# The last down projection with tokens on the partitions, the keys' logarithms on another engine, and an earlier first transpose

## The chip, the cores and the metric

The kernel runs on one core of one Trainium2 chip. The metric is the device time of one execution in microseconds (us); less is better. The core's engines run side by side and meet at semaphores only: TensorE (PE in the profile, its weight loads PEld), VectorE (DVE), ScalarE (ACT), GpSimd (POOL), and SyncE (SP), which issues all DMAs here. TensorE writes to PSUM (eight banks of 512 float32 columns on 128 partitions); VectorE and ScalarE read it.

## The reference, cut to what matters

Two layers of a streaming encoder, over 1024 prompt tokens and 8 x 16 sample tokens (1152 in all, `TOK`), width 1024. What the change touches is the end, and one step of the first mixer:

```python
# ab_mixer (layer 0)
log_f = jnp.logaddexp(jnp.log(lb), jnp.log1p(-lb) + jax.nn.log_sigmoid(fz))
k = (1.0 - lb) * jax.nn.sigmoid(-fz)
...
# conv_ffn, the last part of each layer; D_FF = 2816
y = jnp.einsum('btf,fd->btd', jax.nn.gelu(conv, approximate=False) * gate, w_out)
...
x = x + f.astype(x.dtype)            # residual
...
y = rms_norm(x, norm_final)          # x * rsqrt(mean(x*x) + EPS) * gain, float32
```

With one even layer the lower bound is zero, so the kernel computes log f = min(z,0) - ln(1+exp(-|z|)) and k = exp(log f - z).

## The kernel before, in words

**Layout.** Activations stand transposed: features on the partitions, tokens along them, in three blocks (`NTB`) of 384 tokens (`TB`). The residual is `xs` (eight feature slices of 128). All large products are made of three matmuls of split operands: a rounded high part and a low part (the rest), high x high, high x low, low x high. Activations have `xh`/`xl` or `yh`/`yl`, weights `wh`/`wl`.

**A weight piece** is 128 x 512 values. It goes through a ring of four `raw` buffers: SP loads it (line 422) once the low part of the piece four before is made; POOL multiplies a norm's gain into it (line 2537), or only counts it where there is no gain; ScalarE makes the high part (`high`, line 1974) when TensorE has passed a given tick; VectorE makes the low part (`low`, line 1232). `wh` and `wl` have two places each. TensorE waits for both. A piece of a unit feeds 36 matmuls of 384 columns.

**Order.** Each engine has one program written out by hand; `PLAN` only counts pieces, PSUM groups and ticks so that the semaphore numbers agree. Six banks take the groups in turn; banks 6 and 7 serve norms and small transposes.

**The start.** SP issues three token tiles (`xtok`, tokens on the partitions), then seven small DMAs with the gains as rows (`vrow`), the first pieces, then more tiles. TensorE waits for all seven, turns the tiles with transposes (line 715), and after the fourth group turns the rows into `vec`, which POOL needs for scaling weights.

**The keys.** In the first projection (`ab`) a loop over units j evicts the products on VectorE. At j = 5 VectorE forms `logf` for two halves (line 1314, 128 x 2304 each). POOL subtracts z from it (`log_keys`, line 2581), queued behind its scalings for j = 7. At j = 6 and 7 VectorE scans them (`decay`).

**The end.** The conv-FFN of layer 1 loops over steps of 256 features: four units up (two convolved and gated), one down into `xs`. The last two steps are left to `last_down` (line 683), whose contraction has two halves: `yh`/`yl` and `yh2`/`yl2`. For each quarter of the output features it makes two slices of 128 features by 384 tokens in three groups each. VectorE adds each group to `xs` (line 1245), ScalarE squares it (line 1988), POOL adds the squares into `ssq_b` (line 2543). Then comes the final norm: TensorE sums over the partitions with a matrix of ones (line 697), ScalarE takes the root (line 1993), VectorE the reciprocal (line 1960) and multiplies `xs` by it and by the gain (line 1963). TensorE turns the result (line 1223), ScalarE copies it to `otok` (line 2512), which has two places, and SP stores 128 tokens at a time (line 595). Between them the tails of the convolution are turned (line 1110), copied (`tail_rows`) and stored.

Of the kernel before, what the change touches and what calls it, by code (L numbers as in the profile page):

```python
# [23 lines left out]
P = 128  # L24
# [22 lines left out]
V_MIX, V_FFN, V_FIN, V_OUTG, V_PSC, V_LNG, V_LNB, NVEC = 0, 16, 32, 40, 41, 45, 61, 77  # L47
# [18 lines left out]
for _l in range(2):  # L66
# [10 lines left out]
    PLAN.add(f"f{_l}9", 8, 24, 28)  # L77
PLAN.add("out", 0, 18, 18)
# [3 lines left out]
def build(nc, A, O):  # L82
    ctx = ExitStack()
    with ctx:  # L84
# [38 lines left out]
        y_normed = sem("y_normed")  # L123
# [225 lines left out]
        otok = at("otok", [P, 2, D], F32, slot(8))  # L349

# [4 lines left out]
        def tbs(tb):  # L355
            return slice(tb * TB, (tb + 1) * TB)

# [59 lines left out]
        def _(sp):  # L417
# [17 lines left out]
            def x_tiles(tb):  # L435
                for t in range(3 * tb, 3 * tb + 3):
# [4 lines left out]
                    (V_FIN, A["norm_final"].rearrange("(k p) -> k p", p=P)),  # L441
# [56 lines left out]
            def ffn(l):  # L498
# [27 lines left out]
                n0, _, _ = PLAN.at[f"f{l}9"]  # L526
                last_down(wfo[l], n0, FJ - 4)
# [83 lines left out]
        def _(pe):  # L611
# [94 lines left out]
            pe.wait_ge(rows_loaded, 16 * 7)  # L706
# [371 lines left out]
            def ffn(l):  # L1078
# [22 lines left out]
                n2, g2, _ = PLAN.at[f"f{l}9"]  # L1101
                last_down(n2, g2, done0 + 2 * STEPS, yh2, yl2)

            def turn_tails(l):

                pe.wait_ge(conv_step[l], 9 * FJ)
                pe.wait_ge(rms_ready, NTB * (3 + 2 * l))
# [101 lines left out]
            norm(4, ssq_b)  # L1209
            turn_tails(1)  # L1210

            _, g0, _ = PLAN.at["out"]
            for t in range(NT):
                pe.wait_ge(y_normed, KD * (t // NTB + 1))
                for b in range(2):
                    m = 2 * t + b
                    if m < BANKS:
                        bank = acc_bank(g0 + m, g0 + m)
                    else:
                        pe.wait_ge(y_out, m - (BANKS - 1))  # L1220
                        bank = ps[(g0 + m) % BANKS]
                    for k in range(4):
                        mm = pe.transpose(bank[:, k * P:(k + 1) * P], xs[:, 4 * b + k, t * P:(t + 1) * P], ident[:, :])  # L1223
                    mm.then_inc(pe_tick, 1)
# [3 lines left out]
        def _(dve):  # L1228
            def low(n, s):

                dve.wait_ge(w_high_ready, n + 1)
                dve.tensor_tensor(wl[:, s % 2, :], raw[:, s % RAWS, :], wh[:, s % 2, :].bitcast(F32), ALU.subtract)\  # L1232
                    .then_inc(w_low_ready, 1)
# [81 lines left out]

            def decay(c):
# [1483 lines left out]
```

## Time and profile before

| | |
|---|---|
| median of 3 runs | 3001.09 us (2999.42 to 3002.92) |
| the profiled execution | 3001.59 us, its span 2999.9 us |
| mean granted TensorE clock | 0.985 of full speed |
| TensorE busy | 2876.5 us (96%) |
| VectorE, GpSimd, ScalarE busy | 1558.8, 797.1, 719.0 us |
| DMA | 130.19 MB, 43 GB/s on average |

The span is the time from the first to the last instruction; the execution takes 1.7 us more. Busy time is a sum over the whole kernel and says nothing on where an engine is waited for; for that there are the chain of waits, followed back from the last instruction, and the order of time with the idle time ahead of an instruction in square brackets. Recorded matmul durations overlap, since matmuls are pipelined: 0.69 us are recorded for three of 384 columns, but the next three start 0.52 us later.

### The profile page before, as it was taken

To read this page: it belongs to the slowest core of one execution; us is meant where nothing else is said; L and a number is where in the kernel's file an instruction comes from. 1 tells how busy PE (TensorE), PEld (TensorE's weight loads), DVE (VectorE), ACT (ScalarE), POOL (GpSimd) and SP (SyncE) were. 2 spreads that over 40 slices of the span, in tenths; PEclk is the share of its full clock that TensorE was granted. 3 is DMA by queue.
4 is the path that set the end of the run, shared out by engine and by line. 5 is a ranking of instruction groups with operands and counts; after the bars stand their busy time and mean duration, and the time that the engine had idled before them with its cause. 6 is when DMAs were issued, how large, how long until landed. Compare 5 with 4: busy or idle time off the path is not lost. (4 is left out here: it accounts for less than half of the span.)

```text
span 2999.9 us, 45868 instructions
## 1 busy us (share of the span) xinstructions
PE 2876.5 (96%) x16647; PEld 2823.8 (94%) x16647; DVE 1558.8 (52%) x2787; ACT 719.0 (24%) x1143; POOL 797.1 (27%) x603
## 2 busy tenths in 40 slices
PE   8998987999999999999999999999999999999997
PEld 8898887999999999999999889999999999999996
DVE  4557875454444444446544875555544444444454
ACT  4424453321111111113211211213311111111123
POOL 3233324322222222223211230002422222222223
PEclk9998999999999999999999999999999999999998
DMA  4111001111111111111221101111111111111111
GB/s 138 35 33 45 22 15 32 45 39 43 42 42 38 38 42 42 42 42 39 55 66 42 36 30 42 42 42 39 46 41 40 42 42 39 42 42 42 39 43 70
DMA packets 208066, 130.19 MB, mean 43 GB/s; under 512 B 8851, under 2 KB 205156, under 8 KB 207716
## 3 DMA queue, kind: packets, MB, share of 16 engines
q1 hardware_dynamic: 207972, 128.92, 14.3%
q8 instruction: 61, 1.00, 0.1%
q14 instruction: 33, 0.27, 0.0%
HBM read 120.08 MB, written 8.81 MB: 43 GB/s over the span
## 5 line engine op out<-in xcount | busy, mean ns | idle before, releaser
L634 PE MATMUL bank<-xh,wh 128*128 128x384 f32 x3048 | 701.1, 337 | 27.5 <-DVE wl L1232 26.0
L634 PE MATMUL bank<-xl,wh 128*128 128x384 f32 x3048 | 692.5, 334 | 0.0
L634 PE MATMUL bank<-xh,wl 128*128 128x384 f32 x3048 | 692.4, 334 | 0.0
L2537 POOL TENSOR_TENSOR raw<-raw,vec 128x512 f32<-128x512 f32 x280 | 299.1, 1079 | 1389.2 <-DMA raw<-in_w_in_ffn 897.1
L1974 ACT ACTIVATE wh<-raw 128x512 fp32r<-128x512 f32 x414 | 260.4, 629 | 1654.5 <-PE bank L634 1005.7
L634 PEld LDWEIGHTS bank<-xh,wh 128*128 128x128 f32 x3048 | 539.2, 188 | 43.9 <-issue 40.4
L1232 DVE TENSOR_TENSOR wl<-raw,wh 128x512 fp32r<-128x512 f32 x414 | 322.5, 779 | 474.9 <-ACT wh L1974 474.8
L634 PEld LDWEIGHTS bank<-xl,wh 128*128 128x128 f32 x3048 | 543.6, 188 | 0.0
L634 PEld LDWEIGHTS bank<-xh,wl 128*128 128x128 f32 x3048 | 543.6, 188 | 0.0
L1245 DVE TENSOR_TENSOR xs<-bank,xs 128x384 f32<-128x384 f32 (+1 forms) x672 | 332.8, 550 | 309.4 <-PE bank L659 256.1
L659 PE MATMUL bank<-yh,wh 128*128 128x384 f32 x1152 | 267.6, 340 | 5.5 <-DVE xs L1245 2.8
L659 PE MATMUL bank<-yl,wh 128*128 128x384 f32 x1152 | 266.3, 339 | 0.0
L659 PE MATMUL bank<-yh,wl 128*128 128x384 f32 x1152 | 266.2, 339 | 0.0
L659 PEld LDWEIGHTS bank<-yh,wh 128*128 128x128 f32 x1152 | 208.9, 189 | 6.8 <-issue 6.0
L659 PEld LDWEIGHTS bank<-yh,wl 128*128 128x128 f32 x1152 | 208.7, 189 | 0.0
L659 PEld LDWEIGHTS bank<-yl,wh 128*128 128x128 f32 x1152 | 208.6, 189 | 0.0
L2677 POOL TENSOR_TENSOR gate<-gate,cv 128x1152 f32<-128x1152 f32 x40 | 115.5, 2889 | 234.9 <-DVE xs L1245 212.0
L1238 DVE TENSOR_TENSOR gate<-bank,rstd 128x384 f32<-128x384 f32 x132 | 65.4, 551 | 194.0 <-PE bank L634 194.0
L1238 DVE TENSOR_TENSOR apad<-bank,rstd 128x384 f32<-128x384 f32 x88 | 45.0, 553 | 177.6 <-PE bank L634 177.6
L2543 POOL TENSOR_TENSOR ssq_b<-ssq_b,sq_b 128x384 f32<-128x384 f32 x72 | 82.0, 1139 | 132.5 <-ACT sq_b L1988 124.1
L2683 POOL TENSOR_TENSOR yl<-gate,yh 128x1152 fp32r<-128x1152 f32 x40 | 114.8, 2892 | 0.0
L1700 DVE SCALAR_TENSOR_TENSOR cv<-apad,convc,cv 128x1024 f32<-128x1024 f32 x88 | 112.5, 1278 | 0.0
(263 smaller groups left out, 2972.3 us busy)
## 6 DMA issues: line engine op xcount, KB each, us to landing
raw<-in_w_in_ffn SPq DMA_DIRECT2D x176, 256.0 KB, 2.9
raw<-in_w_out_ffn SPq DMA_DIRECT2D x88, 256.0 KB, 2.6
raw<-in_w_uv_c SPq DMA_DIRECT2D x64, 256.0 KB, 2.8
raw<-in_w_in_ab SPq DMA_DIRECT2D x40, 256.0 KB, 2.9
raw<-in_w_out_c SPq DMA_DIRECT2D x32, 256.0 KB, 2.6
xtok<-in_x_prompt SPq DMA_DIRECT2D x8, 512.0 KB, 6.1
raw<-in_w_out_ab SPq DMA_DIRECT2D x16, 256.0 KB, 2.7
out_y_prompt<-otok SPq DMA_DIRECT2D x8, 512.0 KB, 2.8
```

The costliest lines, as they stand in the source:

```text
L634: mm = pe.matmul(ps[(sg + tb) % BANKS][:, 0:TB], w[:, place, k * P:(k + 1) * P], r[:, kk, tbs(tb)], start=kk == 0 and c == 0, stop=kk == K ...
L659: mm = pe.matmul(ps[(sg + g0 + tb) % BANKS][:, 0:TB], w[:, place, k * 256 + dd * P:k * 256 + (dd + 1) * P], r[:, k, tbs(tb)], start=k == 0 ...
L1232: dve.tensor_tensor(wl[:, s % 2, :], raw[:, s % RAWS, :], wh[:, s % 2, :].bitcast(F32), ALU.subtract)\
L1238: dve.tensor_tensor(dst, ps[bank % BANKS][:, 0:TB], rstd[:, tbs(tb)], ALU.mult)\
L1245: dve.tensor_tensor(xs[:, d, tbs(tb)], ps[sg % BANKS][:, 0:TB], xs[:, d, tbs(tb)], ALU.add)\
L1700: dve.scalar_tensor_tensor(outp, padp[:, j:j + SEQ], col(16 + j), outp, ALU.mult, ALU.add)\
L1974: act.activation(wh[:, s % 2, :], raw[:, s % RAWS, :], ACT.Copy).then_inc(w_high_ready, 1)
L2537: pool.tensor_tensor(r, r, g, ALU.mult).then_inc(w_scaled, 1)
L2543: pool.tensor_tensor(ssq[:, tbs(tb)], ssq[:, tbs(tb)], sq[:, par, :], ALU.add)\
L2677: pool.tensor_tensor(gate[:, c, :], gate[:, c, :], cv[:, c, :], ALU.mult)\
L2683: pool.tensor_tensor(yl[:, c, :], gate[:, c, :], yh[:, c, :].bitcast(F32), ALU.subtract)\
```

## The change

1. The last down projection (layer 1) swaps its operands: a slice of 128 tokens of `yh`/`yl` is the stationary operand, a weight piece of 128 x 512 the moving one, and the product has tokens on the partitions. There are nine token tiles with two column halves each, 18 groups of 12 matmuls. All eight weight pieces are kept (`fin_h`, `fin_l`, `wh`, `wl`, `fin_h2`, `fin_l2`). The first eight groups go over eight banks with their first contraction half, then with their second; the other ten go one after the other.
2. The residual is added in PSUM: four float32 matmuls with a slice of `xs` as the stationary operand and the identity as the moving one, into the same group.
3. The final norm goes by token: ScalarE squares each group with an accumulated sum, two tiny steps make the root, VectorE takes the reciprocal of 128 x 1 and multiplies the PSUM group by it and by the gain along the columns (`fin_gain`, one DMA to all partitions) into `otok`. The additions to `xs`, the squares on `ssq_b`, the norm's matmuls, the scaling of `xs`, the transposes and the copies of before are gone.
4. The tails of layer 1 are turned ahead of the projection instead of behind the norm.
5. `log_keys` is on VectorE at j = 6, between two low parts, instead of on POOL at j = 7.
6. TensorE no longer waits for the rows before the first transpose, only before it turns them; the row of the final gains is not loaded there.

```diff
@@ PLAN @@
-    PLAN.add(f"f{_l}9", 8, 24, 28)
-PLAN.add("out", 0, 18, 18)
+    if _l == 0:
+        PLAN.add("f09", 8, 24, 28)
+PLAN.add("fin", 8, 18, 18)
...
+        FIN_BANKS = tuple((FIN_G + e) % BANKS for e in range(3)) + (6,) + \
+            tuple((FIN_G + e) % BANKS for e in range(3, 6)) + (7,)
@@ sync @@
+                for p in range(8):
+                    a, b, k = p // 4, p // 2 % 2, p % 2
+                    load_piece(FIN_N + p, wfo[1][:, FJ - 4 + 2 * a + k:FJ - 3 + 2 * a + k, b * 512:(b + 1) * 512],
+                               FIN_N + p)
+                sp.wait_ge(pe_tick, FIN_T)
+                sp.dma_start(fin_gain[:, :], A["norm_final"].rearrange("(o d) -> o d", o=1).to_broadcast([P, D]))\
+                    .then_inc(fin_gain_loaded, 16)
@@ tensor, start @@
             pe.wait_ge(ident_ready, 1)
-            pe.wait_ge(rows_loaded, 16 * 7)
...
                 if g == 3:
-                    pe.wait_ge(rows_loaded, 16 * 7)
+                    pe.wait_ge(rows_loaded, 16 * 6)
@@ tensor, end @@
             ffn(1)
-            norm(4, ssq_b)
             turn_tails(1)
...
+            def fin_part(m, a):
+
+                t, b = divmod(m, 2)
+                bank = ps[FIN_BANKS[m % 8]]
...
+                sh, sl = ((yh, yl), (yh2, yl2))[a]
+                for k in range(2):
+                    p = 4 * a + 2 * b + k
...
+                    for c, (w, r) in enumerate(((hi, sh), (hi, sl), (lo, sh))):
...
+                        mm = pe.matmul(bank[:, :], r[:, k, t * P:(t + 1) * P], w,
+                                       start=a == k == c == 0, stop=a == k == 1 and c == 2)
+                return mm
...
+            def fin_residual(m):
...
+                for k in range(4):
+                    pe.matmul(bank[:, k * P:(k + 1) * P], xs[:, 4 * b + k, t * P:(t + 1) * P], ident[:, :],
+                              start=False, stop=False)
+
+            for m in range(8):
+                fin_part(m, 0)
+                fin_residual(m)
+            for m in range(8):
+                fin_part(m, 1).then_inc(pe_tick, 1)
+            for m in range(8, 2 * NT):
+                fin_part(m, 0)
+                fin_residual(m)
+                fin_part(m, 1).then_inc(pe_tick, 1)
@@ vector @@
+                if j == 6:
+                    log_keys(0)
+                    log_keys(1)
                 low(2 * j + 2, 2 * j + 2)
...
-                        low(n + 2 * u + 2, sn + 2 * u + 2)
+                        if l and u == 3 and isinstance(s, int) and s:
+                            for p in range(4):
+                                fin_low(p)
...
+            dve.wait_ge(fin_gain_loaded, 16)
+            for t in range(NT):
+                dve.wait_ge(fin_rms, t + 1)
+                inv = fin_sums[:, t, 2:3]
+                dve.reciprocal(inv, inv).then_inc(fin_inv, 1)
+                if t >= 2:
+                    dve.wait_ge(y_stored[t % 2], 16 * (t // 2))
+                dve.wait_ge(fin_inv, t + 1)
+                for b in range(2):
+                    c = slice(b * 512, (b + 1) * 512)
+                    dve.scalar_tensor_tensor(otok[:, t % 2, c], ps[FIN_BANKS[(2 * t + b) % 8]][:, :], inv,
+                                             fin_gain[:, c], ALU.mult, ALU.mult).then_inc(y_out, 1)
@@ scalar @@
+                        for p in range(4):
+                            fin_high(p, 0)
+                        fin_high(4, tick + 13)
+                        y_high(s, yh2, (0,))
+                        fin_high(5, tick + 16)
+                        tail_rows(1)
+                        y_high(s, yh2, (1,))
+                        fin_high(6, tick + 16)
+                        fin_high(7, tick + 16)
...
                 for b in range(2):
                     m = 2 * t + b
+                    act.wait_ge(pe_tick, FIN_T + m + 1)
+                    if m:
+                        act.wait_ge(fin_squared, m)
+                    act.activation(fin_sq[:, :], ps[FIN_BANKS[m % 8]][:, :], ACT.Square,
+                                   accum_out=fin_sums[:, t, b:b + 1]).then_inc(fin_squared, 1)
+                act.wait_ge(fin_squared, 2 * t + 2)
+                act.activation(fin_sums[:, t, 3:4], fin_sums[:, t, 1:2], ACT.Identity, bias=eps_c, scale=1.0 / D)\
+                    .then_inc(fin_bias, 1)
+                act.wait_ge(fin_bias, t + 1)
+                act.activation(fin_sums[:, t, 2:3], fin_sums[:, t, 0:1], ACT.Sqrt, bias=fin_sums[:, t, 3:4],
+                               scale=1.0 / D).then_inc(fin_rms, 1)
@@ gpsimd @@
-                if j == 7:
-                    log_keys(0)
-                    log_keys(1)
```

## Rows read from the trace of the kernel before

**Rows 1.** The page: head, and busy us, share and instructions of TensorE.
```profile
span 2999.9 us, 45868 instructions
...
PE 2876.5 (96%) x16647; PEld 2823.8 (94%) x16647; DVE 1558.8 (52%) x2787; ACT 719.0 (24%) x1143; POOL 797.1 (27%) x603
```

**Rows 2.** The chain that ended last, from 2900 us: start, us, what.
```profile
2910.68 46.87 PE bank L683 x268
...
2971.48 4.32 DVE xs L1963 x8
```

**Rows 3.** TensorE in order of time, the last projection: start, us, instructions.
```profile
2910.52 0.69 PE L683 MATMUL bank<-yh,wh 128*128 128x384 f32 x3
...
2960.32 0.69 PE L683 MATMUL bank<-yh,wl 128*128 128x384 f32 x3
```

**Rows 4.** All engines in order of time, the keys in the first projection.
```profile
101.11 5.02 DVE L1314 SCALAR_TENSOR_TENSOR work<-work 128x2304 f32<-128x2304 f32 x2
...
103.73 12.80 POOL L2581 TENSOR_TENSOR work<-work 128x2304 f32<-128x2304 f32 x2 [10.47 <-DVE work L1314]
...
106.04 11.04 DVE L1232 TENSOR_TENSOR wl<-raw,wh 128x512 fp32r<-128x512 f32 x2
...
111.71 1.30 PE L634 MATMUL bank<-xh,wh 128*128 128x384 f32 x3 [5.46 <-DVE wl L1232]
...
119.65 0.68 PE L634 MATMUL bank<-xh,wh 128*128 128x384 f32 x3
```

**Rows 5.** All engines in order of time, the start.
```profile
8.44 2.79 PE L715 MATMUL bank<-ident,xtok 128*128 128x128 f32 x12 [8.44 <-DMA vrow<-in_c_ln_bias]
...
16.00 0.61 PE L715 MATMUL bank<-ident,xtok 128*128 128x128 f32 x3
```

**Rows 6.** TensorE in order of time, four plain float32 products inside a unit.
```profile
247.42 1.11 PE L876 MATMUL bank<-work,ones 128*128 128x128 f32 x8
248.28 0.77 PE L788 MATMUL bank<-xh,wh 128*128 128x384 f32 x3
248.89 0.34 PE L788 MATMUL bank<-xl,wh 128*128 128x384 f32 x1
```

**Rows 7.** ScalarE's groups by line and shape: busy us, mean ns | idle before.
```profile
L1988 ACT ACTIVATE sq_b<-xs 128x384 f32<-128x384 f32 x72 | 35.9, 519 | 41.9 <-POOL ssq_b L2543 22.0 <-DVE xs L1245 19.9
...
L2512 ACT ACTIVATE otok<-bank 128x512 f32<-128x512 f32 x18 | 10.3, 596 | 13.1 <-PE bank L1223 7.9 <-DMA out_y_prompt<-otok 5.0
...
L1993 ACT ACT_TABLE_LOAD x5 | 6.4, 1283 | 0.1
...
L2007 ACT ACTIVATION_READ_ACCUMULATOR xsq<-xtok 128x1 f32 x9 | 1.8, 202 | 0.0
L2140 ACT ACTIVATE ebp<-work 128x4 f32<-128x4 f32 x8 | 1.6, 196 | 0.0
```

**Rows 8.** Line 1483 alone: duration ns min/median/max, first and last start.
```profile
L1483 DVE SCALAR_TENSOR_TENSOR work<-work,vec x9: 743/751/1214, 252.5 to 470.7; 128x512 f32<-128x512 f32 x9
```

**Rows 9.** All engines in order of time, ScalarE's last copies.
```profile
2995.68 1.09 ACT L2512 ACTIVATE otok<-bank 128x512 f32<-128x512 f32 x2
```

**Rows 10.** VectorE in order of time, in the last gated unit.
```profile
2905.21 0.69 DVE L1232 TENSOR_TENSOR wl<-raw,wh 128x512 fp32r<-128x512 f32 x1 [5.16 <-ACT wh L1974]
```

**Rows 11.** Token tiles' DMAs, issued before 3 us and from 6 to 9 us.
```profile
L437 SPq DMA_DIRECT2D xtok<-in_x_prompt x3: 397/421/432, 0.8 to 1.7; - x3
...
DMA to landing us min/median/max: 3.7/4.5/5.5
...
L437 SPq DMA_DIRECT2D xtok<-in_x_prompt x3: 432/433/758, 6.1 to 7.4; - x3
...
DMA to landing us min/median/max: 5.7/6.5/7.8
```

**Rows 12.** The recurrence's stretch: length, busy us (count), granted clock, DMA share, GB/s.
```profile
200.00:500.00 300.00, 256.27 (x1643) 242.54 (x1642) 220.77 (x352) 139.09 (x274) 107.22 (x89) 0.93 0.10 29
```

**Rows 13.** TensorE's weight loads by line and shape: those of the last transposes.
```profile
L1223 PEld LDWEIGHTS bank<-ident,xs 128*128 128x128 f32 x72 | 12.4, 197 | 9.1 <-DVE xs L1963 9.1
```

More of the change, by code:

```diff
@@ L1638, in _, with finish_down @@
                 abo(i)
-            def finish_down(n0, g0, t0, k, last):
+            def finish_down(n0, g0, t0, k):
                 def lows(d):
-                    if not last:
-                        for tb in range(NTB):
-                            x_low(24 * k + NTB * d + tb, d, tb)
+                    for tb in range(NTB):
+                        x_low(24 * k + NTB * d + tb, d, tb)
                 def adds(d):
@@ L1759, in ffn @@
                 y_last(1)
-                n2, g2, t2 = PLAN.at[f"f{l}9"]
-                finish_down(n2, g2, t2, 2 + 2 * l, l == 1)
+                if l == 0:
+                    n2, g2, t2 = PLAN.at["f09"]
+                    finish_down(n2, g2, t2, 2)
+                else:
+                    for p in range(5, 8):
+                        fin_low(p)
             ffn(0)
@@ L2318, in _, with finish_down @@
                 abo(i)
[L2320 removed]
+            def finish_down(n0, g0, t0, k):
                 for q in range(4):
@@ L2323, in finish_down @@
                         p = n0 + 2 * q + dd + 2
-                        if p < PIECES:
-                            high(p, p, t0 + 7 * q + (7 if dd else 1))
+                        high(p, p, t0 + 7 * q + (7 if dd else 1))
                         for tb in range(NTB):
                             m = 6 * q + NTB * dd + tb
-                            finished(24 * k + m, 2 * q + dd, tb, g0 + m, sq_b, not last)
+                            finished(24 * k + m, 2 * q + dd, tb, g0 + m, sq_b)
                         for tb in range(NTB):
@@ L2357, in ups @@
                             gelu(1, 2 * s + 1)
-                        if p >= 8 and isinstance(s, int) and s:
-                            y_high(s, yh2, (p - 8,))
+                    if not isinstance(s, int) or s == 0:
+                        high(n + 8, sn + 8, tick + 13)
+                        high(n + 9, sn + 9, tick + 16)
+                    elif l == 0:
+                        for c in range(2):
+                            high(n + 8 + c, sn + 8 + c, tick + 13 + 3 * c)
+                            y_high(s, yh2, (c,))
+                    else:
+                        for p in range(4):
[7 more added lines that the diff above has]
+                        fin_high(7, tick + 16)
                 n0, g0, t0 = PLAN.at[f"f{l}0"]
@@ L2707, in ffn @@
                         y_low(STEPS - 2)
-                n2, _, _ = PLAN.at[f"f{l}9"]
-                linked(pool.memset(ssq_b[:, :], 0.0))
-                scale_weights(n2, 0, 4, None)
-                scale_weights(n2 + 1, 0, 4, None)
-                finish_down(n2, 2 + 2 * l, V_MIX + KD if l == 0 else None)
+                if l == 0:
+                    n2, _, _ = PLAN.at["f09"]
+                    linked(pool.memset(ssq_b[:, :], 0.0))
+                    scale_weights(n2, 0, 4, None)
+                    scale_weights(n2 + 1, 0, 4, None)
+                    finish_down(n2, 2, V_MIX + KD)
+                else:
+                    for p in range(8):
+                        scale_weights(FIN_N + p, 0, 4, None)
             ffn(0)
```

143 lines of the change are left out of this document (83 added, 60 removed).

## The prediction

> **What bounds the kernel now.** I read the page's busy times first: TensorE is busy for 2876.5 us of a span of 2999.9 us [rows 1]. So only two kinds of place can give much: where TensorE idles, and what comes after its last real product. Second, the chain of waits over the last 100 us: the last down projection (the matmuls of line 683) is one unbroken TensorE piece up to 2957.6 us, and behind it comes a chain through every engine in turn: squares, POOL's sums, one reciprocal and eight scalings (4.3 us together) for each of three token blocks, transposes, copies, stores [rows 2]. Third, I read the order of time around the projection: it starts at 2910.52 us, its last three matmuls start at 2960.32 us [rows 3]. With 0.52 us for those three it is over at 2960.84 us, so 39.1 us of the span are the tail. Last, the waits of TensorE before 510 us, which led to the two other places of the diff: 5.46 us at 111.7 us, ended by VectorE's low part of a weight piece [rows 4], and 8.44 us at the very start, ended by the DMA of the last small row of gains [rows 5].
>
> **The last projection, part by part.** Before, it is 288 matmuls of 384 columns in 50.32 us [rows 3], 174.7 ns each. 384 columns at the granted full clock of 2.4 GHz are 160.0 ns, so 14.7 ns come on top. After, 18 groups (9 token tiles, 2 column halves) have 12 matmuls of 512 columns each: 216, with the same 110592 columns. No row shows this kind of operand 512 wide. From below the columns alone give 213.3 ns, 46.1 us in all; from above, an excess in proportion gives 232.9 ns, 50.3 us. I take the excess as fixed for each matmul, since each has its own weight load in both: 213.3 + 14.7 = 228.0 ns, 49.3 us.
>
> The residual comes back as TensorE work: 18 x 4 products of 128 columns in plain float32. The nearest row is a group of four plain float32 products of 128 columns (eight records, since each takes two passes): from 247.42 to 248.28 us, 0.86 us for four [rows 6]. 18 x 0.86 = 15.5 us. Behind those four the next three wide matmuls took 0.61 us (248.28 to 248.89) rather than 0.52: a switch costs 0 to 0.09 us. I take half, 18 x 0.045 = 0.8 us. The four turned tails of the convolution move ahead of the projection: about four times 0.11 us from the same row, 0.45 us. The norm's three products and the 72 output transposes go; they lay wholly in the tail.
>
> Sum on TensorE: 0.45 + 49.3 + 15.5 + 0.8 = 66.05 us, so its stream ends at 2910.52 + 66.05 = 2976.6 us. Its drain shows as the difference between 0.69 us recorded for three and 0.52 us of pace [rows 3]: 0.17 us.
>
> Behind the last group stands this chain, for one token tile of 128 only. ScalarE squares 512 columns of PSUM (a copy of that form 0.60 us) and reads its accumulator (0.20 us); two tiny ScalarE steps, each as the 128 x 4 form at 0.20 us [rows 7], each with some 0.05 us to the next by the gaps in the chain; a tiny reciprocal, which I price the same, 0.2; two VectorE steps of 512 columns, for which the row of that form gives a median of 0.75 us [rows 8], with 0.05 for what a read of PSUM may add; then the store. The last of ScalarE's copies of before ends at 2996.77 us and the span at 2999.9 us [rows 1, 9]: 3.1 us. Together 0.17 + 0.85 + 0.50 + 0.2 + 1.55 + 3.1 = 6.4 us. New end 2983.0 us, 16.9 us earlier.
>
> What hides the rest: the eight weight pieces now need eight highs and lows that mostly sit earlier, four of them within the last gated unit. There VectorE's next low comes only at 2905.2 us, after 5.16 us of idleness [rows 10]; four lows are 4 x 0.69 = 2.8 us. On ScalarE the four highs need no tick; the fourth also needs its transfer, which can leave only when the low ahead of that idleness is done, at 2900.0 us, so even with the 5.5 us that a far larger transfer took to land at the start [rows 11] it ends before 2907 us, and TensorE wants that piece at about 2913 us: 6 us of cover. Behind the waiting fourth low are queued the product for the last gate, and behind ScalarE's fourth high its rounding; they need to be ready only when the second half of the contraction starts, eight groups (8 x 2.27 = 18 us) after 2910.5. The broadcast of the final gains on SP stands behind all weight loads and is 20 us early. The tail copies of ScalarE (0.76 us for four) delay the last highs by that much, inside the same 18 us. For each token tile ScalarE needs about 2.3 us and VectorE 1.8 us, beside 2.7 us of TensorE for two groups in the opening eight and 7.2 us later, so neither becomes the bound; the store of tile t-2 is waited for by VectorE, which has that slack.
>
> **The keys' logarithms.** Before, two POOL steps run from 103.73 us for 12.8 us, and two VectorE lows which alone take 0.69 us each take 11.04 us beside them [rows 4]. TensorE stands for 5.46 us, then restarts at half clock: the 36 matmuls from 111.71 to 119.65 us take 7.94 us, where 36 x 0.1747 = 6.29 us is the pace. After, VectorE does the two subtractions between those lows. Its row for two steps of that size with both inputs in SBUF is 5.02 us [rows 4]. The first low then ends at 106.04 + 0.69 = 106.73 us, and TensorE stands about 0.5 us, a tenth of the idle time that came before the fall of its clock. The second ends at 106.73 + 5.1 + 0.69 = 112.5 us; TensorE needs it at 106.8 + 6.29 = 113.1 us. So that unit ends at 113.1 rather than 119.65 us: 6.6 us. POOL may slip one gain scaling (1.04 us) between VectorE's steps and turn the spare 0.5 us into a wait of 0.6; I take 6.4 us and 5.8 to 6.7 as bounds. The scans that follow on VectorE keep their place behind the unit's evictions, and whatever wait they cause stays. The Trainium skill's page "SBUF — State Buffer", section "Who interferes with whom", says that a VectorE instruction with two SBUF inputs and a GpSimd instruction that reads SBUF exclude each other for a whole instruction. The 11.04 us row agrees; by the same rule the moved steps still collide with POOL's scalings, which is the bound just given.
>
> **Turning at once.** The first turn waits until 8.44 us for the rows' DMA [rows 5]. The third token tile, issued at 1.7 us, lands 5.5 us later, at 7.2 us [rows 11]. So four turns and all behind them can start 1.2 us earlier; the second block of tokens, however, lands on its own schedule, near 15.2 us (issued at 7.4, 7.8 us to land [rows 11]), against a first turn of it at 16.00 us less the matmul in flight, some 15.8 us [rows 5]. So 0.6 us of the 1.2 come through for certain. I take 0.8, bounds 0 and 1.2.
>
> **The sum.** 16.9 + 6.4 + 0.8 = 24.1 us. The profiled run took 3001.59 us, its span 2999.9; the median of the runs is 3001.09, 0.5 us lower. 3001.1 - 24.1 = 2977.0 us.
>
> **The rivals.** (a) The gain at the keys is given back. The stretch from 200 to 500 us is full of short TensorE waits, and its mean granted clock is 0.93 [rows 12], so 0.07 x 300 = 21 us of clock are lost in it by a pattern of gaps that a shift may change; I allow a sixth of it, 3.5 us, either way, and if the whole 6.4 us were absorbed the time is 2983.4 us. Against it: every wait there hangs on engines that all start earlier. 0.10.
> (b) Squares and roots alternate on ScalarE, and each change reloads a table. The row for a load is 1283 ns, five for the five norms' roots, and none stands at the 72 squares of line 1988 [rows 7], although they follow other functions; but no square follows a root directly here. Reloads in each tile would be hidden except the last: 2977.0 + 1.3 = 2978.3 us. 0.10. The Trainium skill's page "ScalarE: Activation LUTs", section "Table sets: the hidden batching unit", tells one to batch by set and lists relu, copy, identity and abs, not square, as in every set; by that rule each tile would reload, and no row here settles it.
> (c) The float32 products of the residual show their weight loads, which the moved operand no longer shares: a pass takes 0.107 us [rows 6] and a plain float32 load 0.197 us [rows 13], so 8 x 0.09 = 0.72 us more for each group, 18 x 0.72 = 13 us, 2990 us. Against it: the four priced above had their loads too [rows 6]. 0.05.
> (d) Slower than before: 512-wide products of the split operands run at two cycles for a column, as the float32 passes do (0.107 us for 128 columns [rows 6]). 427 ns each instead of 228 are 216 x 0.199 = 43 us more: 3020 us. It decides from 228 + 24.1/0.216 = 340 ns. Against it: nothing in the 384-wide rows depends on width. 0.03.
> (e) No excess at 512 columns: 3.2 us less, 2973.8 us. 0.06.
>
> **How the numbers follow.** Forecast 0.66, with its own range 2972 to 2981 from the bounds above: 46.1 to 50.3 us for the products, 0 to 1.6 for the switches, 5.8 to 6.7 and 0 to 1.2 for the two early edits, and 3.5 either way for the clock, not all at one end. The range reaches to (a), (b) and (e) and leaves out (c) and (d): 2968 to 2985. About 0.2%, 6 us, is what a measurement of this kernel can tell from no change. Only (d) ends above; a few mishaps together could cancel: faster 0.95, same 0.02, slower 0.03.
>
> **What would show it.** TensorE without a gap from 2890 us on its old scale to the last product; 216 records of 512 columns spaced 0.228 us; the residual's four products in 0.86 us; the last store issued about 3.2 us after TensorE's last product; no table load after the first root; TensorE's stop at the keys 0.5 us and its clock full there; first turn at about 7.3 us. The forecast is wrong if the spacing is above 0.24 us, if ScalarE or VectorE holds a bank so that TensorE waits at the ninth group, or if the recurrence takes the 6 us back.

## The result, and the profile after

The changed kernel took 2978.19 us (median of 4 runs, 2977.78 to 2982.36) against 3000.47 us for the one before beside it (4 runs, 2999.42 to 3002.92): a ratio of 0.9928, with a 95% interval from 0.9911 to 0.9945. That is 22.3 us less (16 to 27 by the interval); 24.1 had been forecast, and 2977.0 us. The profiled execution took 2978.5 us, its span is 2976.7 us against 2999.9 [rows 1], 23.2 us less.

First the page's head and TensorE's share. TensorE does nearly the same work in a shorter span, and the other engines' sums have fallen, which tells nothing of where the time went:

```profile
span 2976.7 us, 45853 instructions
...
PE 2872.6 (96%) x16641; PEld 2814.1 (95%) x16641; DVE 1537.2 (52%) x2765; ACT 711.9 (24%) x1152; POOL 760.2 (26%) x576
```

Second, the chain of waits behind the last gated unit (start, us, what). It is TensorE alone up to 2970.3 us and then one short chain for one token tile, where before it went on through every engine for 39 us [rows 2]:

```profile
2904.08 0.44 PE bank L1148 x4
...
2922.75 12.30 PE bank L1271 x54
2935.06 0.89 PE bank L1280 x8
2935.95 2.77 PE bank L1271 x12
...
2970.29 0.02 issue
2970.31 0.70 ACT fin_sq L2622 x2
...
2971.03 0.30 ACT fin_sums L2625
...
2971.36 0.30 ACT fin_sums L2628
...
2971.68 0.17 DVE fin_sums L2049
...
2971.95 0.75 DVE otok L2055
```

Line 1148 turns the tails, 1271 is the projection, 1280 the residual, 2622 the squares. The projection now begins at 2904.5 us, not 2910.5 [rows 3]. The list of TensorE's waits is empty from 2886 us to the end. Behind the chain's last row come VectorE's second half and the store: the second half ends at 2973.4 us and the span at 2976.7.

Third, all engines in order of time at the keys; each row answers to one of [rows 4]:

```profile
105.38 0.68 DVE L1299 TENSOR_TENSOR wl<-raw,wh 128x512 fp32r<-128x512 f32 x1
...
105.98 5.02 DVE L1392 TENSOR_TENSOR work<-work 128x2304 f32<-128x2304 f32 x2
106.21 0.76 PE L669 MATMUL bank<-xh,wh 128*128 128x384 f32 x3 [0.62 <-DVE wl L1299]
...
109.03 2.87 POOL L2653 TENSOR_TENSOR raw<-raw,vec 128x512 f32<-128x512 f32 x1 [10.56 <-DMA raw<-in_w_in_ab]
...
110.92 1.53 DVE L1299 TENSOR_TENSOR wl<-raw,wh 128x512 fp32r<-128x512 f32 x1
...
112.59 0.77 PE L669 MATMUL bank<-xh,wh 128*128 128x384 f32 x3
...
113.78 5.79 DVE L1398 TENSOR_TENSOR_SCAN work<-resetm,work 128x1152 f32<-128x1152 f32 x2
...
115.47 1.70 POOL L2653 TENSOR_TENSOR raw<-raw,vec 128x512 f32<-128x512 f32 x1 [3.56 <-DMA raw<-in_w_in_ab]
...
120.31 0.77 PE L669 MATMUL bank<-xh,wh 128*128 128x384 f32 x3 [1.20 <-DVE wl L1299]
```

TensorE stands 0.62 us where it stood 5.46, and the unit whose end was at 119.65 us ends at 112.59. One GpSimd scaling of 1.04 us did slip between VectorE's steps: GpSimd spent 2.87 us on it and VectorE 1.53 on a low part of 0.69, and it stayed in the spare time, since nothing stands at 112.59 us.

A second scaling falls into VectorE's two scans, and that costs something. Before, the scaling ended 0.2 us after the scans had begun:

```profile
120.91 5.11 DVE L1320 TENSOR_TENSOR_SCAN work<-resetm,work 128x1152 f32<-128x1152 f32 x2
```

In both kernels VectorE starts them 1.2 to 1.3 us after TensorE's unit (113.78 - 112.59, 120.91 - 119.65), but now they take 5.79 us, and the scaling beside them 1.70 instead of 1.04. The low part behind the scans comes later by that much, and TensorE's stop for it is 1.20 us, where it was 0.69.

Fourth, TensorE at the start. The first turn now waits for the token tile itself:

```profile
8.02 2.79 PE L749 MATMUL bank<-ident,xtok 128*128 128x128 f32 x12 [8.02 <-DMA xtok<-in_x_prompt]
```

The account of the two profiled spans, then: 0.7 us at the start (first unit at 49.27 instead of 49.93 us), 6.4 at the keys' unit, of which 0.5 is given back behind the scans, and in the tail 16.6 (from the unit's end to the span's end 72.8 us, before 89.4). 0.7 + 5.9 + 16.6 = 23.2. This works because the stretches that the change doesn't touch are equally long in these two profiles; the table below shows that they need not be.

### The profile page after: what moved, and what is told of

It reads as the page before. It is cut to its first block and busy times, and to the rows that moved or that the text cites. A ratio compares the mean times of both kernels' runs of the same rounds, so it can differ in the third digit from the quotient of the medians.

```text
span 2976.7 us, 45853 instructions
## 1 busy us (share of the span) xinstructions
PE 2872.6 (96%) x16641; PEld 2814.1 (95%) x16641; DVE 1537.2 (52%) x2765; ACT 711.9 (24%) x1152; POOL 760.2 (26%) x576
## 5 line engine op out<-in xcount | busy, mean ns | idle before, releaser
L669 PE MATMUL bank<-xh,wh 128*128 128x384 f32 x3048 | 700.5, 337 | 23.2 <-DVE wl L1299 21.8
L1299 DVE TENSOR_TENSOR wl<-raw,wh 128x512 fp32r<-128x512 f32 x406 | 308.5, 760 | 457.6 <-ACT wh L2066 457.5
L1318 DVE TENSOR_TENSOR xs<-bank,xs 128x384 f32<-128x384 f32 (+1 forms) x648 | 321.0, 550 | 291.3 <-PE bank L694 256.2
L2448 ACT ACTIVATE cv<-cv 128x1152 f32<-128x1152 f32 x44 | 51.3, 1166 | 222.1 <-DVE cv L1782 222.1
```

The costliest lines, as they stand in the source:

```text
L669: mm = pe.matmul(ps[(sg + tb) % BANKS][:, 0:TB], w[:, place, k * P:(k + 1) * P], r[:, kk, tbs(tb)], start=kk == 0 and c == 0, stop=kk == K ...
L1318: dve.tensor_tensor(xs[:, d, tbs(tb)], ps[sg % BANKS][:, 0:TB], xs[:, d, tbs(tb)], ALU.add)\
L2448: act.activation(cv[:, c, :], cv[:, c, :], ACT.Gelu).then_inc(gelu_done[l], 1)
```

## The experiments

A table of landmarks from TensorE's order of time serves several of them. It has the start of the first unit's products, then five lengths that together make up the rest of the span: to the first product of the recurrence (about 142 us), from there to the first product of the out projection (about 453 us), from there to the first unit of the feed-forward part (about 570 us), from there to the end of the last unit, and the tail behind it.

| kernel | median us | ratio to before [95%] | first unit | to the recurrence | recurrence | out projection | to the tail | tail |
|---|---|---|---|---|---|---|---|---|
| before | | | 49.93 | 98.7 | 311.0 | 117.0 | 2333.8 | 89.4 |
| after | 2978.19 | 0.9928 [0.9911, 0.9945] | 49.27 | 93.0 | 310.9 | 117.0 | 2333.8 | 72.8 |
| tail_alone | 2986.94 | 0.9950 [0.9934, 0.9967] | 48.59 | 98.7 | 310.8 | 117.0 | 2337.0 | 72.5 |
| keys_alone | 2998.47 | 0.9986 [0.9977, 0.9996] | 50.00 | 93.0 | 314.0 | 116.5 | 2336.5 | 88.2 |
| keys_back | 2987.57 | 0.9952 [0.9935, 0.9969] | 49.05 | 99.0 | 312.8 | 116.4 | 2336.4 | 72.5 |
| rows_first | 2983.50 | 0.9935 [0.9919, 0.9952] | 49.03 | 93.0 | 314.2 | 116.5 | 2336.6 | 72.8 |
| after_again | 2977.91 | 0.9920 [0.9904, 0.9937] | 49.41 | 92.9 | 314.1 | 116.4 | 2336.8 | 72.8 |
| keys_pieces | 2984.61 | 0.9940 [0.9924, 0.9957] | 48.94 | 97.8 | 312.8 | 116.4 | 2336.2 | 72.5 |
| no_residual | 2966.18 | 0.9881 [0.9865, 0.9898] | 48.06 | 93.0 | 313.8 | 116.4 | 2336.3 | 56.9 |
| reload | 2979.53 | 0.9932 [0.9915, 0.9948] | 49.63 | 93.0 | 310.7 | 117.0 | 2333.5 | 74.1 |
| sums_spread | 2972.34 | 0.9907 [0.9890, 0.9923] | 47.52 | 93.0 | 313.9 | 107.9 | 2334.7 | 72.5 |
| both | 2970.57 | 0.9899 [0.9882, 0.9916] | 48.59 | 93.0 | 314.0 | 107.9 | 2334.7 | 71.6 |
| both_again | 2969.80 | 0.9899 [0.9882, 0.9915] | 48.85 | 92.9 | 310.6 | 108.1 | 2336.0 | 71.6 |

`tail_alone`, `keys_alone`, `keys_back` and `rows_first` were timed against a before of 3002.61 us on their chip, the others against 2999.6 to 3000.5 us, so kernels are compared by ratio. The interval of a ratio is about 0.3% wide, 10 us, and so the landmarks tell the small edits apart, not the totals.

**One part alone, and one part undone.** `keys_alone` is the kernel before with the subtractions moved to VectorE; `tail_alone` is the changed kernel with the subtractions back on GpSimd and the wait for the rows back at the start, `keys_back` with the subtractions alone, `rows_first` with the wait alone. The row of the final gains, which is no longer loaded at the start, comes back in none of them, so `rows_first` and `tail_alone` wait for six rows, before and `keys_alone` for seven:

```diff
@@ keys_back (and tail_alone) @@
-                if j == 6:
-                    log_keys(0)
-                    log_keys(1)
+            def log_keys(c):
+                z, f = work[:, 4 + 2 * c:6 + 2 * c, :], work[:, 20 + 2 * c:22 + 2 * c, :]
+                pool.wait_ge(logf_ready, c + 1)
+                pool.tensor_tensor(z, f, z, ALU.subtract).then_inc(logf_used, 1)
...
+                if j == 7:
+                    log_keys(0)
+                    log_keys(1)
@@ rows_first (and tail_alone) @@
+            pe.wait_ge(rows_loaded, 16 * 6)
```

> The changed kernel with the keys' logarithms back on POOL and the rows' wait back at the start: only the new projection is left. My theory, three independent parts: the projection is worth 16.6 us (in the changed trace the units end at 2903.9 us and the span 72.8 us later, before they end at 2910.4 us and the span 89.5 us later), so 3000.5 - 16.7 = 2983.8 us, ratio to before 0.9944. Rival, the parts help each other (a kernel that is ahead early loses part of it in the recurrence): less than 2 us of the early edits arrives in the whole kernel, and this one comes to within 2 us of the changed kernel, 2979 to 2981 us.

> The kernel before with the two subtractions of the keys on VectorE between two low parts at j = 6, and nothing else changed. My theory: TensorE's stop of 5.46 us shrinks to about 0.6 us and its clock does not fall, so the unit ends 6.4 us earlier and 6 us of that reach the end: 2994.3 us, ratio 0.9980. Rival, the recurrence between 130 and 510 us gives it back through other gaps: 2999 to 3001 us, and the start of the first unit of the FFN is where it was.

> The changed kernel with the subtractions back on POOL at j = 7. My theory: TensorE stands about 5.5 us for a low part that runs beside POOL's step and restarts at half clock, 6.0 to 6.5 us more than the changed kernel, 2984.5 us, ratio to before 0.9947. Rival (given back in the recurrence): 2978 to 2980 us.

> The changed kernel with TensorE waiting for the six rows before its first transpose. The changed trace begins its first transpose at 8.02 us, ended by the token tile, before at 8.44 us, ended by the last row; the row that is gone makes the six rows land about 0.4 us earlier. My theory: the waits for rows and tile now end nearly together, so this costs 0 to 0.4 us, first transpose at 8.0 to 8.4 us, 2978.4 us. Rival, removing the wait is what gave the 0.66 us seen at 99 us: 2978.9 us, and the eviction that stands at 99.04 us in the changed trace comes at 99.7 us.

The tail alone: by ratio 0.0050 x 3000 = 15 us (10 to 20), where 16.9 was forecast. By the landmarks it is 72.5 us long, against 89.4 in before and 88.2 in `keys_alone`, whose tail is the old one: 15.7 to 16.9 us. The old tail itself varies, since ScalarE's last copies waited there until a store had left `otok`; that is 0.9 of the 1.2 us. The chain of waits has that store in both, first before, then `keys_alone`:

```profile
2992.13 3.53 DMA out_y_prompt<-otok
```

```profile
2991.36 2.61 DMA out_y_prompt<-otok
```

The keys: the three profiles with the two uncut subtractions on GpSimd have 98.7 to 99.0 us to the recurrence, all nine with them on VectorE 92.9 or 93.0, so 5.7 to 6.0 us reach the recurrence each time. The expectation for `keys_back` was 6.0 to 6.5 us; its ratio is 7 to 10 us above the changed kernel's, with an uncertainty of 7. The place is the same as before, as all engines in order of time show for `keys_back`:

```profile
102.85 12.81 POOL L2694 TENSOR_TENSOR work<-work 128x2304 f32<-128x2304 f32 x2 [10.48 <-DVE work L1387]
105.16 11.05 DVE L1299 TENSOR_TENSOR wl<-raw,wh 128x512 fp32r<-128x512 f32 x2
110.83 1.30 PE L669 MATMUL bank<-xh,wh 128*128 128x384 f32 x3 [5.46 <-DVE wl L1299]
```

The wait for the rows: in `rows_first` the first turn starts at 8.17 us, ended by the last row, inside the 8.0 to 8.4 of the theory. The first unit starts at 49.03 us, earlier than after (49.27), and the eviction that the rival put at 99.7 us comes at 98.80, so putting the wait back costs nothing that can be seen. What moves the first unit is, in part, the clock: over 8 to 30 us it is 1.00 in `tail_alone`, `no_residual` and `sums_spread`, whose first units are at 47.5 to 48.6 us, and 0.92 in the ten others (48.6 to 50.0). Among those ten the two that load seven rows are the 49.93 and 50.00. Whether the seventh row is what counts, two profiles don't show.

In total, though, `keys_alone` gained only 4 us (0.0014 x 3000, with 1 to 7 by the interval), and its recurrence is 3 us longer than those of before and after. The next run asked whether the edit does that.

**The changed kernel again, on another chip.**

> The kernel after the change, unchanged, as the base for the other runs made on this chip, where the runs of the first group came out some 2 us longer than sums from the first two profiles gave. Theory: the end is worth 16.6 us, the start 0.7, the keys 6.4 at TensorE, of which the recurrence (200 to 500 us) takes 2 to 3 back in some executions: 2978 to 2981 us, and the stretch from the first product of the attention at 142 us to the first half unit of the out projection is 311 or 314 us. Rival: the longer times of the first group are losses of those edits themselves; then this kernel is again at 2978.2 us within 0.5.

Its median is 2977.91 us, which fits the rival's number (2978.2 within 0.5) and lies just below the theory's range. But the 2 us by which the first group was longer are there in its before as well (3002.61 us against 3000.47), so they are not a loss of those edits. Its profiled execution, the longest of the four (2984.20 us), has a span of 2982.4 us with a recurrence of 314.1 us: the same program as the one with 310.9. The first place where they part is TensorE at 168.5 us, behind two rows of sixteen products of 16 columns. TensorE in order of time, and the stretch from 162 to 182 us (its granted clock is the column with 1.00 or 0.91), in the first profile of this kernel:

```profile
168.53 0.77 PE L822 MATMUL bank<-xh,wh 128*128 128x384 f32 x3
169.14 0.70 PE L822 MATMUL bank<-xl,wh 128*128 128x384 f32 x3
```

```profile
162.00:182.00 20.00, 19.41 (x110) 16.62 (x109) 8.74 (x13) 1.67 (x4) 7.65 (x5) 1.00 0.09 26
```

and the same two views in this one:

```profile
168.68 1.31 PE L822 MATMUL bank<-xh,wh 128*128 128x384 f32 x3
169.79 1.16 PE L822 MATMUL bank<-xl,wh 128*128 128x384 f32 x3
```

```profile
162.00:182.00 20.00, 19.90 (x107) 17.63 (x105) 7.71 (x11) 1.35 (x4) 7.65 (x5) 0.91 0.09 26
```

From these three products to the next it is 1.11 us instead of 0.61: TensorE runs there at its lower level (1.2 GHz) in one execution and not in the other. So one program has both a recurrence of 311 us and one of 314, and a difference of that size between two profiles can't be laid on an edit. The stretch behind the out projection varies as much, 2333.8 and 2336.8 us in this program. There the longer profile has a stop that the shorter one has not:

```profile
1756.94 0.45 PE L694 MATMUL bank<-yh,wh 128*128 128x384 f32 x1 [2.78 <-DVE ut L1311]
```

With the out projection, which is 0.6 us shorter there, the two account for the 5.7 us between the spans. The eight executions of this program run from 2976.89 to 2984.20 us.

Does the edit make the slower course of the recurrence more likely? Of the nine profiles with the keys on VectorE, six show about 314 us and three 311. In these six the granted clock over 158 to 190 us is 0.95, in the seven others 1.00. None of the four profiles with the keys on GpSimd is among the six; two show 311 us and two 312.8. If the edit had nothing to do with it, four such profiles in a row would still come up about once in twenty draws (worked out from 6 of 13). So it may cost some 2 us on average (6/9 of 3.2), and 13 profiles don't settle it.

**The subtractions on GpSimd, in pieces.**

```diff
+                for h in range(2):
+                    for part in range(2):
+                        o = slice(part * 576, (part + 1) * 576)
+                        z, f = work[:, 4 + 2 * c + h, o], work[:, 20 + 2 * c + h, o]
+                        ins = pool.tensor_tensor(z, f, z, ALU.subtract)
+                ins.then_inc(logf_used, 1)
```

> The kernel after the change, but the subtractions for the keys' logarithms are back on GpSimd at j = 7, each of the two cut into four of 128x576. Theory: a GpSimd step and a VectorE step with all operands in SBUF exclude each other for one instruction, so a VectorE low part of 0.69 us waits for one piece of about 1.6 us (12.80 / 8) and not for all; TensorE's stop near 112 us is then 1.2 to 2 us where the uncut form has 5.5, and the time is within 2 us of the kernel after the change (2979 to 2981). Rival: GpSimd holds the port until its row of steps is through, or the wait is for its result; then the stop stays 5.5 us and the time is 6 us above it (2985).

All engines in order of time:

```profile
102.74 16.50 POOL L2697 TENSOR_TENSOR work<-work 128x576 f32<-128x576 f32 x8 [10.56 <-DVE work L1387]
...
105.05 3.72 DVE L1299 TENSOR_TENSOR wl<-raw,wh 128x512 fp32r<-128x512 f32 x2
...
107.09 0.76 PE L669 MATMUL bank<-xh,wh 128*128 128x384 f32 x3 [1.82 <-DVE wl L1299]
...
119.20 6.18 POOL L2650 TENSOR_TENSOR raw<-raw,vec 128x512 f32<-128x512 f32 x3
...
123.19 0.77 PE L669 MATMUL bank<-xh,wh 128*128 128x384 f32 x3 [3.37 <-ACT wh L2063]
```

and the durations of the eight pieces (ns, min/median/max):

```profile
L2697 POOL TENSOR_TENSOR work<-work x8: 1426/1652/3682, 102.7 to 115.6; 128x576 f32<-128x576 f32 x8
```

The mechanism is as the theory had it: beside pieces VectorE's two low parts take 3.72 us, not 11, and TensorE's stop is 1.82 us, so what VectorE waits for is one GpSimd instruction, not GpSimd's queue. The time is as the rival had it (2984.61 us, against 2985), for a reason neither named. GpSimd waits in turn: a piece takes 1.43 us where nothing is in its way, 1.86 and 1.88 where it starts beside one of the two low parts, and 3.65 and 3.68 beside VectorE's long steps, the `logf` step and the scans. So its row grew from 12.8 to 16.5 us, the gain scalings queued behind it begin at 119.20 us (115.62 in `keys_back`), and ScalarE's high part and TensorE stop for them, 3.37 us at 123.2 us. It is 97.8 us to the recurrence: of the 5.7 to 6.0 us, this keeps 1. Moving the work off GpSimd bought a free queue as much as a free port.

**The projection without the residual.**

```diff
@@ both loops @@
                 fin_part(m, 0)
-                fin_residual(m)
```

> The kernel after the change without the residual: the 72 float32 products are left out, so the output lacks it. Theory: TensorE bounds the end, and a residual group costs the 0.89 us that lie between its first product and the next wide one: 18 x 0.89 = 16.0 us less, TensorE's end at 2954 us on the scale of the kernel after the change, and still no wait of TensorE behind 2905 us. Rival: without it the chain for a token tile on ScalarE and VectorE (square, root, reciprocal, scaling; about 4.6 us for two groups) sets the pace against TensorE's 5.5 us for a tile, or the banks come free too late: waits at the ninth group and 8 to 13 us less only.

The chain of waits of this kernel:

```profile
2907.76 0.44 PE bank L1148 x4
2908.20 49.82 PE bank L1271 x216
2958.04 0.70 ACT fin_sq L2620 x2
```

216 products in one piece of 49.82 us are 230.6 ns each (with the drain of the last), and no wait is in them. From the first turned tail to TensorE's end it is 50.3 us against 66.2 (2904.08 to 2970.29 us): 15.95 us for the residual, 16.0 expected. The ratio gives 0.9920 - 0.9881 = 0.0039, 12 us (5 to 19 by the two intervals); the profiled spans of this kernel and of `after_again` differ by 17.9, of which 1.4 lie ahead of the first unit and 15.9 in the tail. The tail is TensorE-bound, and stays so 16 us below.

**A table reload for each tile.**

```diff
+                act.activation(fin_other[:, t:t + 1], eps_c, ACT.Gelu)
```

> The kernel after the change with one tiny Gelu on ScalarE ahead of each token tile's squares, so that a table has to be changed twice in a tile (2 x 1.28 us by the row of the norms' roots). This prices the rival in which squares and roots live in different tables. Theory: in the tiles before the last both reloads lie in ScalarE's idle time (about 5.5 us a tile needed beside 7.3 us of TensorE), so only what stands behind TensorE's last product counts: one reload ahead of the last root, +1.3 us. Rival: the reloads hold PSUM banks in the opening eight groups, where results come every 1.39 us, so that TensorE waits: +5 us or more.

Table loads by line (2618 the added Gelu, 2630 the root), then ScalarE's last tile in order of time:

```profile
L2630 ACT ACT_TABLE_LOAD x9 | 11.5, 1283 | 0.2
L2618 ACT ACT_TABLE_LOAD x8 | 10.3, 1283 | 0.1
```

```profile
2966.83 0.20 ACT L2618 ACTIVATE fin_other<-vec 128x1 f32<-128x1 f32 x1
2966.94 0.58 ACT L2624 ACTIVATE fin_sq<-bank 128x512 f32<-128x512 f32 x1
...
2971.25 1.28 ACT L2630 ACT_TABLE_LOAD   x1
2972.55 0.29 ACT L2630 ACTIVATE fin_sums<-fin_sums 128x1 f32<-128x1 f32 x1
```

Seventeen loads (21.8 us of ScalarE) where there had been one cost 1.3 us in the chain, that of the last root, and the tail grew from 72.8 to 74.1 us. (The medians, 2979.53 and 2977.91 us, agree but could not tell so little.) No load stands at a square, neither behind the Gelu here nor, in the changed kernel, behind a root: there the profile has one load in the whole tail, at the first root.

**GpSimd's other long row.** In the changed kernel the largest stop of TensorE left is 12.66 us at 492.9 us. GpSimd, TensorE and ScalarE in order of time:

```profile
467.52 22.37 POOL L2749 TENSOR_TENSOR xs<-xh,xl 128x1152 f32<-128x1152 f32 x8 [19.96 <-DVE ol L1698]
...
490.88 0.52 ACT L2085 ACTIVATE sq_e<-xs 128x384 f32<-128x384 f32 x1 [14.36 <-POOL ssq_e L2659]
491.31 1.13 ACT L2066 ACTIVATE wh<-raw 128x512 fp32r<-128x512 f32 x2
...
492.90 1.32 PE L1102 MATMUL bank<-oh,wh 128*128 128x384 f32 x3 [12.66 <-DVE wl L1299]
```

Eight sums hold GpSimd, a square waits for its buffer, and the weight's high part is queued behind the square. The edit spreads the sums:

```diff
+            for k in range(3):
+                xs_sum(k)
...
+            for p in range(4, 8):
+                scale_weights(n0 + p, 0, 4, None)
+            abo(0)
+            for p in range(4, 8):
+                xs_sum(p - 1)
+                scale_weights(n0 + p, 1, 4, None)
+            xs_sum(7)
+            abo(1)
```

> The kernel after the change; besides, GpSimd's eight sums xh + xl into xs ahead of the attention's out projection (22.4 us in a row from 467.5 us) are spread: three, then the first step's squares, then the other five between the weight pieces of the second step. In the kernel after the change ScalarE's square waits 14.4 us for GpSimd there, the high part of a weight piece is queued behind it, TensorE stands 12.66 us at 492.9 us and then runs at half clock for some 13 us. Theory: this stop and its clock go: 12.7 less some 1 us of remaining wait plus half of 13: 15 to 19 us less, 2959 to 2964 us. Rival: the VectorE step that takes 7.15 us beside the sums (it takes 1.6 alone) then sits in the way of the weights' low part, or the sums are late for the second step: a stop of 4 to 8 us stays with its half clock and the gain is 4 to 8 us (2970 to 2974).

> As sums_spread, and at the end two tiny edits: the step that adds epsilon works on the sum of the first column half, so that it comes before the last square (0.33 us less in the last chain), and the last token tile is stored in two halves, the first beside VectorE's second half (0 to 0.4 us less). Theory: 0.3 to 0.7 us below sums_spread, seen only in the chain behind TensorE's last product: 5.7 to 6.1 us instead of 6.4. Rival: the second DMA of the last tile is issued behind the first and lands later than one whole DMA did: 0 to 0.5 us worse at the store.

> As both, with another order of GpSimd's work in the second step of the out projection: all eight sums of xs stand before the count of the third weight piece, and the squares of the step's first half before the count of the fourth. In sums_spread the square there waited 11.2 us because GpSimd stood 6.5 us at the count of a piece not yet landed, with a sum and the squares queued behind; TensorE stood 3.53 us at 510.7 us and the granted clock was 0.88 over the 14 us around. Theory: that stop goes and its clock with it, 3.5 + 1.7 = 5.2 us below both: 2964 to 2967 us. Rival: the stop only moves, to the low part of the fourth piece or to the next step, since the high part still waits for the transfer: within 2 us of both (2969 to 2972).

`both` also works epsilon into the sum of the first column half, ahead of the last square, and stores the last tile in two halves. `both_again` changes GpSimd's order in the second step once more: all sums, then the count of the third piece, squares, the count of the fourth. `sums_spread` gained 4 us over `after_again` by ratio, within the noise. By the landmarks its out projection is 107.9 us long, where all kernels without the edit have 116.4 to 117.0: 8.5 to 9.1 us, where the theory had 15 to 19 and the rival 4 to 8. TensorE's stops there, in `sums_spread` and in `both_again`:

```profile
481.93 0.79 PE L1102 MATMUL bank<-oh,wh 128*128 128x384 f32 x3 [0.38 <-DVE wl L1299]
510.69 0.80 PE L1102 MATMUL bank<-oh,wh 128*128 128x384 f32 x3 [3.53 <-DVE wl L1299]
```

```profile
494.00 7.06 DVE L1327 TENSOR_TENSOR xl<-xs,xh  x3
...
502.62 0.77 PE L1105 MATMUL bank<-ph,wh 128*128 128x384 f32 x3 [3.68 <-DVE wl L1302]
```

The stop of 12.66 us is 0.38, and a new one of 3.53 us has come a step later: 12.66 - 0.38 - 3.53 = 8.75. The clock had been mis-sized too: over the 13 us behind the old stop it was 0.82, which is 2.3 us, not half of 13. In `both_again` the stop only moved 8 us earlier and the out projection is not shorter (108.1 us), as its rival had it: VectorE's `xl` takes 7.06 us beside the sums, and the low part is queued behind it. The two last edits of the tail showed in the chain: TensorE's end to the span's end is 5.2 us in `both` and `both_again`, 6.1 in `sums_spread`, 6.4 after. That is 0.9 below `sums_spread`, more than the 0.3 to 0.7 expected: 0.32 is the step with epsilon, and the other 0.6 lies at the store, which had been given 0.4 at most. `both_again` at 2969.80 us (2969.59 to 2972.42) is below every run of the changed kernel (2976.89 at the least) and of the one before.

## Why the prediction was right, point by point

- **The projection's products.** 228.0 ns was the term, the columns at full clock plus a fixed excess. The piece of 54 gives 12.30 / 54 = 227.8 ns, the whole 216 without the residual 230.6, the granted clock over 2904 to 2970 us is 1.00. An excess in proportion to the columns would be 232.9 ns; the piece of 54 has 14.5 ns of excess and the 216 in one piece 16.5 without the drain, where proportion would give 19.6, so most of it belongs to the matmul. Neither rival on this (none, or two cycles for a column) has anything left.
- **The residual.** Forecast 0.86 + 0.045 us a group, 16.3 us in all; the rows show 0.89 in the chain, and the experiment 15.95. The exposed weight loads of rival (c) don't appear.
- **TensorE's stream.** 66.05 us and 0.17 of drain forecast, 66.4 found: the first turned tail starts at 2903.91 us, and the chain has TensorE's end, drain included, at 2970.29.
- **The chain behind it.** 6.2 us forecast without the drain, 6.4 found in this profile and 6.1 in `tail_alone` and `sums_spread`, from terms that erred both ways, so the close sum is in part luck. The squares with their accumulator took 0.70, not 0.85, and VectorE's two halves 1.41, not 1.55. The two tiny ScalarE steps took 0.30 each, not 0.20: they read their bias from a 128 x 1 tile, and the added Gelu of `reload`, equally small but without one, takes 0.20. From VectorE's end to the span's end it was 3.3 us, not 3.1.
- **Cover.** Eight highs and lows, the tail copies, the broadcast of the gains and the tiles' store cost nothing: TensorE has no wait behind 2886 us. The fin_gain transfer is issued at 2904.11 us and first needed some 20 us later.
- **Tables, rival (b).** One load in the tail, at the first root. The Trainium skill's page "ScalarE: Activation LUTs", section "Table sets: the hidden batching unit", lists functions that every set has, and square is not among them; the trace says more, since squares follow both Gelus and roots with no load. Had the rule held for squares, `reload` prices it at 1.3 us.
- **The keys.** 6.4 us forecast at that unit and 6.4 measured (119.65 - 112.59 less the 0.66 of the start). What was not worked out is the stop behind the scans, 0.5 us more than before; "whatever wait they cause stays" was wrong by that much. The prediction let GpSimd's scalings collide with the moved steps but not with the scans that follow: with the edit they take 5.79 or 5.80 us in all nine profiles, beside a scaling of 1.70 us or more, and with the two uncut steps on GpSimd 4.99 to 5.25. The Trainium skill's page "SBUF — State Buffer", section "Who interferes with whom", holds: the exclusion lasts one instruction, as `keys_pieces` shows (two low parts take 3.72 us beside pieces, 11.05 beside whole steps).
- **Rival (a)**, the recurrence takes the gain back: not in this pair of profiles, whose recurrences are equal. What exists is a spread of 3 us between executions of one program, inside the 3.5 us allowed for the clock; that the edit makes the longer course more frequent is neither shown nor excluded. A recurrence of 314 us in the profile after would have left 20 of the 23.2 us, and that it was 311 is luck.
- **The start.** 0.8 forecast, 0.66 found, and this agreement is luck. The first turn still waited for its tiles until 8.02 us, and they were forecast for 7.2, so it came 0.4 us earlier rather than 1.2. Over all profiles the first turn starts between 7.64 and 8.18 us with the edit (nine) and between 8.17 and 8.73 without (four), 0.5 us on average; but the first unit, where a gain would have to arrive, starts anywhere from 47.5 to 50.0 us, and `rows_first` has it no later than the changed kernel. The tiles' landing and the clock of the first 30 us were taken as fixed, and both move by as much as the edit is worth. That the missing wait gains anything is not shown.
- **The total.** 24.1 us less 0.5 (scan), 0.3 (tail: 16.6, not 16.9) and 0.1 (start) is the 23.2 of the two spans. The medians give 22.3, within what the measurement can tell. So the size of the tail and the mechanism at the keys are confirmed part by part; the medians alone could not separate 24 from 20.

## What to carry to other kernels

Behind TensorE's last product, count the chain for the smallest piece of output that can be finished alone: swapping the operands so that a tile of tokens comes out whole turned 39 us behind the last product into 6, though it cost 16 us of extra TensorE work. Moving a long step off a shared helper engine is worth what its queue holds up as well as what its port does, so look at both before cutting the step into pieces instead. After an edit of a few microseconds, compare landmarks along the same engine in the two traces, since totals of one program differ by up to 7 us between executions, and check first that the stretches the edit doesn't touch are equally long.

## What the runs showed of the hardware that was not expected

- The granted clock of one stretch can fall in one execution of a program and not in the next: 1.00 and 0.91 over 162 to 182 us, after the same 32 products of 16 columns. Over 8 to 30 us it is 1.00 in three of the thirteen profiles and 0.92 in ten.
- The waiting goes both ways. A GpSimd piece of 128x576 takes 1.43 us at the least, and 3.68 beside VectorE's scans; eight in a row took 16.5 us, where two uncut steps took 12.8. VectorE's scans lose as well: 6.99 us beside the pieces, 5.79 beside one scaling, 4.99 in `keys_back`.
- Square needs no table change behind Gelu or behind the root, and a reload before each root is 1283 ns, hidden wherever TensorE has the next group in hand.
